# Sample rows' attention dealt out over the last 17 steps of a hybrid layer's main attention

## The reference

```python
(q, kv, gate, z_a, q_g, k_g, v_g, a_low, z_b, merge) = split(h @ w_in)
# prompt and sample rows alike:
o_nsa = gate0 * attend(q, compressed) + gate1 * attend(q, selected) + gate2 * attend(q, window)
# each head of the gated linear attention, chunks of 32 (prompt) or 4 (sample) tokens:
b = cumsum(log_sigmoid(a_low @ a_up + a_b) / 16)
q_dec, k_inv, k_tail = q * exp(b), k * exp(-b), k * exp(b_last - b)
o = tril(q_dec @ k_inv.T) @ v + q_dec @ S;  S = exp(b_last) * S + k_tail.T @ v
y = x + (sigmoid(g_a) * ((o_nsa * silu(z_a)) @ w_ba)
         + sigmoid(g_b) * ((rms_norm(o) * silu(z_b)) @ w_bb)) @ w_out
```

## Time and profile before

| | us |
|---|---|
| median of 3 runs | 1400.13 |
| lowest and highest | 1395.86, 1402.26 |
| profiled execution, its own time | 1407.33 |
| its span | 1405.3 |
| PE busy in the span | 1324.4 (94%) |
| DVE, ACT, POOL busy | 613.7 (44%), 621.4 (44%), 148.5 (11%) |
| mean granted TensorE clock | 0.974 of full |

### The profile page before, as it was taken

How to read it: one execution, slowest core, us unless ns; L and a number is a source line. 1 busy time by engine, 2 the same in 40 slices (tenths; PEclk the granted TensorE clock), 3 DMA queues, 4 the chain that set the end, 5 groups by cost and what they waited for, 6 DMA issues and landing times.

```text
span 1405.3 us, 23475 instructions
## 1 busy us (share of the span) xinstructions
PE 1324.4 (94%) x9533; PEld 1190.3 (85%) x9533; DVE 613.7 (44%) x1365; ACT 621.4 (44%) x1063; POOL 148.5 (11%) x182
## 2 busy tenths in 40 slices
PE   5999989998989999999999999999778889999998
PEld 4999989998978889988888899889556678999876
DVE  5211145634733344434333333332489766453342
ACT  5212235442332555655565567564558542221121
POOL 2100001103200000000000000001710270000000
PEclk9999999999989999999999999999779999999999
DMA  7251453411212212212122112212645555443231
GB/s 199 63 170 33 138 118 91 128 51 59 67 36 56 62 57 62 63 56 62 57 77 62 48 56 61 73 42 67 232 154 191 198 174 177 153 139 104 90 127 60
DMA packets 141307, 137.38 MB, mean 98 GB/s; under 512 B 27121, under 2 KB 125761, under 8 KB 141137
## 3 DMA queue, kind: packets, MB, share of 16 engines
q1 hardware_dynamic: 138416, 127.47, 29.8%
q0 software_dynamic: 2784, 8.43, 2.1%
HBM read 98.02 MB, written 41.88 MB: 100 GB/s over the span
## 4 chain that ended last, share of the span: by engine, by line
PE 65%; DVE 4%; ACT 2%; issue 2%; POOL 1%; DMA 1%; another core or an unknown queue 0%; POOLq 0%; SPq 0%; DVEq 0%; ACTq 0%
PE ps L218 37%; PE ps L2285 6%; PE ps L1176 5%; PE ps L1210 5%; PE ps L1192 4%; PE ps L1225 1%; PE ps L2196 1%; POOL oL L2334 1%; PE ps L2176 1%; DVE S L2392 1%; PE ps L2200 1%; PE ps L2293 1%; PE ps L1146 0%; DVE sP L1361 0%
## 5 line engine op out<-in xcount | busy, mean ns | idle before, releaser
L218 PE MATMUL ps<-hH,wH 128*128 128x352 f32 (+1 forms) x1320 | 443.0, 336 | 7.9 <-ACT stg L334 4.9
L218 PE MATMUL ps<-hH,wL 128*128 128x352 f32 (+1 forms) x1320 | 428.2, 324 | 0.0
L218 PE MATMUL ps<-hL,wH 128*128 128x352 f32 (+1 forms) x1320 | 427.5, 324 | 0.0
L218 PEld LDWEIGHTS ps<-hH,wH 128*128 128x128 f32 (+1 forms) x1320 | 250.0, 189 | 38.3 <-issue 26.9
L218 PEld LDWEIGHTS ps<-hL,wH 128*128 128x128 f32 (+1 forms) x1320 | 251.0, 190 | 2.2 <-issue 1.9
L218 PEld LDWEIGHTS ps<-hH,wL 128*128 128x128 f32 (+1 forms) x1320 | 250.0, 189 | 0.3
L1361 DVE CUSTOM_DVE_ANT_0 sP<-ps,dist,stat 128x256 f32<-128x256 f32 (+3 forms) x116 | 58.5, 542 | 203.4 <-issue 132.2
L205 DVE TENSOR_TENSOR wL<-w_raw,wH 128x1024 fp32r<-128x1024 f32 (+1 forms) x55 | 67.8, 1233 | 162.0 <-ACT wH L197 162.0
L1429 ACT ACTIVATE pPT<-ps 128x512 f32<-128x512 f32 x74 | 44.1, 596 | 181.2 <-PE ps L1192 181.1
L334 ACT ACTIVATE stg<-ps 128x352 f32<-128x352 f32 x132 | 60.8, 462 | 98.5 <-PE ps L218 90.0
L1472 ACT ACTIVATE sP<-sP,stat 128x640 f32<-128x640 f32 (+7 forms) x128 | 93.0, 729 | 4.4 <-DVE stat L1361 3.8
(11 more groups left out here) (378 smaller groups left out, 2100.8 us busy)
## 6 DMA issues: line engine op xcount, KB each, us to landing
w_raw<-in_w_in SPq DMA_DIRECT2D x46, 512.0 KB, 3.9
p_spill<-stg SPq DMA_DIRECT2D x132, 176.0 KB, 1.8
zt<-p_spill SPq DMA_DIRECT2D x24, 528.0 KB, 5.0
w_raw<-in_w_in SPq DMA_DIRECT2D x17, 256.0 KB, 3.8
gvT<-p_spill SPq DMA_DIRECT2D x8, 528.0 KB, 6.6
rq<-p_spill SPq DMA_DIRECT2D x8, 528.0 KB, 6.2
x_all<-in_x_prompt SPq DMA_DIRECT2D x8, 512.0 KB, 9.6
m_raw<-in_w_branch_b SPq DMA_DIRECT2D x8, 512.0 KB, 5.5
```

What stands on the lines that cost most here:

```text
L218: mm = nc.tensor.matmul(ps[0:t.m, bank, 0:NF], w[:, c % 2, t.m * k:t.m * k + t.m], x[:, k, NF * n:NF * n + NF], start=(k == 0 and i == 0), ...
```

## The change

The 93 units are dealt out over steps 0 to 48 instead of 0 to 65 (M0 = 49): 44 steps have two and five have one, where the before had 69 units in these 49 steps and 24 in the last 17. The sample rows' attention and head 0's elementwise part are no stage of their own any more:

- The two stages of the compressed branch go into steps 12 to 14 and 19 to 21 (C_AT), into columns 352 to 511 of the banks that the units use: `borrow` waits for the last unit's output, and `held` makes the second unit after it wait until DVE has read what was lent.
- The four stages with pages, the turning of pages, the gate products of heads 0 to 2 and head 0's elementwise part go into steps 49 to 65 (t = 0 to 16), in banks 2 and 3, which no unit needs there.
- In these 17 steps DVE's order is another one: a stage's bias, `copies(m)` with its `drain`, `output`, `weigh`, and only then `score(m+3)`, then a piece of head 0.
- The turning of head 0's values moves into `core(0)`, before its state products; SP loads these values after step 65's transposes. Page loads, biases, masks and the memory layout follow.

```diff
+                if u in held:
+                    pe.wait_ge(sem(held[u][0]), held[u][1])
                 ring.products(c, n, bank, hH, hL).then_inc(sem("u_done"), 1)
...
-            return UA * (m + 1) // ncut - UA * m // ncut
+            return UA * (m + 1) // M0 - UA * m // M0 if m < M0 else 0
...
+        M0 = 49
+        C_AT = (12, 19)
+        TURNS = {1: (1, 2), 2: (3,), 3: (4,), 5: (5, 6), 6: (7,), 7: (8,), 9: (9, 10), 10: (11,), 11: (12,), 13: (13, 14),
+                 14: (15,)}
...
+        def borrow(pe, what, u, read):
+
+            last = unit["pe"] - (1 if what == "scores" else 2)
+            unit_out(pe, last)
+            held[last + 2] = (read, u + 1)
+            lent[what, u] = 3 - last % 2
+            return lent[what, u]
...
+            def turn_page(c):
+
+                n, b = divmod(c, NB)
+                if b == 0:
+                    pe.wait_ge(sem(f"kp_loaded{n % 2}"), 16 * NB * (n // 2 + 1))
+                    if n >= 1:
+                        pe.wait_ge(sem("z_scored"), n + 2)
...
+                if t in (7, 11, 15):
+                    pe.wait_ge(sem("z_scored"), t // 4 + 3)
+                    decay_gate(pe, *((1, 0), (1, 2), (2, 1))[t // 4 - 1])
+                for c in TURNS.get(t, ()):
+                    turn_page(c)
+                if value_unit(t):
+                    turn_probs(value_unit(t))
...
+            def tail_step(m):
+
+                t = m - M0
+                if t % 4 == 3:
+                    z_score(score_unit(t - 1))
+                if value_unit(t):
+                    copy_probs(value_unit(t))
+                copies(m)
+                if value_unit(t):
+                    output(value_unit(t))
+                for j in range(4 * R):
+                    if cut_of[4 * j + 3, 0] == m:
+                        weigh(j)
+                if m + LA < ncut:
+                    score(m + LA)
+                head_part(t)
...
+                if m - 1 in C_AT:
+                    z_score(C_AT.index(m - 1))
+                if m - 2 in C_AT:
+                    copy_probs(C_AT.index(m - 2))
                 if m + LA < ncut:
                     score(m + LA)
+                if m - 2 in C_AT:
+                    output(C_AT.index(m - 2))
...
+            def tail_step(m):
+
+                t = m - M0
+                for c in TURNS.get(t, ()):
+                    copy_key(c)
...
+                copies(m)
...
+                if t % 4 == 3:
+                    z_probs(score_unit(t - 1))
+                if t == 3:
+                    log1p(act, 0)
```

More of the change, by code:

```diff
@@ L291, in hybrid_step @@
         NU = 3 * NP
+        held = {}
         unit = {"pe": 0, "act": 0, "dve": 0, "sp": 0}
@@ L1100, in hybrid_step @@
                 holder[spot[n] + k] = (n, k)
+        ZU = [(0, 2), (1, 2)] + [(gp, br) for gp in range(2) for br in range(2)]
+        PU = [(gp, br) for gp, br in ZU if br < 2]
+        cleared_free = list(cleared)
         UA = NU - 39
@@ new lines, in head_part @@
+            def head_part(t):
+                if t == 1:
+                    minus_abs(dve, 0)
+                elif t == 5:
+                    log_sigmoid(dve, link, 0)
+                elif t == 6:
+                    sums(dve, 0)
+                elif t == 7:
+                    tails(dve, link, 0)
+                elif t == 9:
+                    queries(dve, link, 0)
+                elif t == 10:
+                    inverses(dve, 0)
+                elif t == 11:
+                    keys(dve, link, 0)
+                elif t == 13:
+                    spans(dve, link, 0)
+                    for n in range(NSTG):
+                        dve.wait_ge(sem(f"p_stored{n}"), 16 * ((NU - n + NSTG - 1) // NSTG))
+                elif t == 14:
+                    later_queries(link, 0)
+                elif t == 15:
+                    minus_abs(dve, 1)
```

1131 lines of the change are left out of this document (571 added, 560 removed).

## The result

| kernel | median, us | runs | ratio to before | 95% interval |
|---|---|---|---|---|
| before | 1398.40 | 1395.86 to 1402.26, 4 runs | 1 | |
| changed | 1450.18 | 1440.69 to 1451.64, 4 runs | 1.0351 | 1.0307 to 1.0395 |

A forecast was written before the change was run, and what follows sets the result against it. PE was taken to bound the main attention, with units filling every wait. 91.7 + 117.7 + 17.2 = 226.6 us against 209.8, plus 17.2 for compressed stages and 7 for their clock, gave +41: 1441 us, range 1405 to 1456.

The forecast's parts named there:

- 24 units moved: Units leaving steps 49 to 65 become second units of earlier steps: 24 x 3.82 = 91.7 us.
- Compressed stages: Steps 12 to 14 and 19 to 21: 2.2 us of PE work plus three uncovered waits per stage, 17.2 us.
- The walk through the 17 steps: Steps 49 to 65 without units: 74 us PE work, 30 waits and 13 clock, 117.7 us.
- t = 3: Step 52: PE waits 3.8 us for ACT's copy, drain, score and bias before page 4 may overwrite the bank.
- t = 0: Step 49: PE waits 2.7 us while DVE makes a score, weigh and step 48's copy.
- t = 4: Step 53's transposes wait 1.3 us more, as the logarithm and two exponentials stand on ACT before them.
- The clock: Four waits in the last 17 steps are each followed by 6 to 10 us at 1.2 GHz, costing 13 us.
- The end: Step 65's transposes to the first state product: 17.2 us, PE waiting for head 0's values until 10.3; bounds 14 and 21.
- rival 3: Late loads and longer chains, with 12 us more for half clock: +57 to +65, about 1460 us; chance 8%.
- Drain at a table load: Logarithm's two table loads: a skill's 1.38 us drain each would add 2.8 us, making +44; left out of the forecast.
- Rival 1: PE's work alone counts, hand-overs hidden: 185 us against 210, -25, 1375 us; chance 9%.
- The signs: Window to step 49 about 526 + 24 us; 17 steps PE 75% busy, clock near 0.8, named idle times; above 0.95 wrong.

The follow-up runs named there:

- units_49: Kernel before with its projection units dealt over the first 49 steps, none in the last 17, sample stretch left in place; 1447.69 us, ratio 1.0325.
- c_out_first: Changed kernel with DVE doing the sample unit's output before the scores of step m+3 in steps 14 and 21; 1436.67 us, ratio 1.0233.
- c_ungated: Changed kernel with the compressed sample units at steps 25 and 32 instead of 12 and 19; 1442.71 us, ratio 1.0251.
- all4: Changed kernel with compressed units at steps 25 and 32, PE, DVE and ACT lists reordered, gated head's logarithm at t = 6 before spread weights' copy; 1400.52 us, 0.9987.
- log1p_late: Changed kernel with ACT's exponential and logarithm of the first gated head at the end of t = 4 instead of t = 3; 1452.94 us, ratio 1.0323.

## Why the prediction was right, point by point

Forecast 1441, measured 1450.18, in the range of 1405 to 1456 and on the forecast's side. By the trace of before, the forecast was a span of 1405.3 + 41 = 1446.3, and the changed kernel's trace has 1439.0, 7.3 less, of which 5.35 lie ahead of the first transposes, in code that did not change. So the forecast is 7 us too high between the two traces and 9 us too low at the median. The sum against the profiled execution of the changed kernel:

| term | forecast, us | trace after, us |
|---|---|---|
| first transposes to the last unit, with step 48's rest | 429.2 + 91.7 + 17.2 + 7 = 545.1 | 542.95 (404.11 to 947.06) |
| the 17 steps, to the last transposes | 117.7 | 114.6 |
| of them waits | 30 | 32.5 |
| of them clock | 13 | about 8 (114.6 - 32.5 - 74) |
| last transposes to the state product | 17.2 | 18.2 |
| everything behind | 356.8 | 359.2 |

- **24 units moved, 91.7.** Right. units_49 shows it alone: 517.97 us from the first transposes to the last unit, with 2.4 us of idle, where 429.2 + 91.7 less some 3 us of step 48 behind the last unit was forecast.
- **Compressed stages, 17.2, of which 15 are waits.** The three kinds were forecast as 2.9, 1.5 and 3.1 us and measured as 3.1, 1.4 and 3.2 on the mean. c_out_first and c_ungated each took one of them away. Not foreseen was the fourth (2.5 us at step 9): I had dealt with two units per step as with one.
- **The walk through the 17 steps.** The waits of t = 3 (3.8 forecast, 3.65 measured), t = 7 (6.4; 6.19) and t = 11 (2.2; 2.63) were right to half a microsecond. Three were too low: t = 0 (2.7; 3.84), t = 15 (1.1; 1.94) and t = 4 (1.3; 3.74), where the walk took half clock behind t = 3's wait to hide a part. No half clock came there in this execution. In that of c_ungated, with the same code there, it came, and the wait at t = 4 is 2.01. t = 10 and 12 were too high (3.1 and 2.7; 2.1 and 2.1). The list adds up by errors of both signs, so that 30 against 32.5 is in part luck.
- **The clock, 13.** The step that was mis-sized: about 8. I took the waits of t = 0, 3, 7 and 10 to be followed by 6 to 10 us at 1.2 GHz. In the profiled execution half clock follows those of t = 0, 4, 7 and 12, and for 3 to 5.5 us; none follows that of t = 10, nor the one before t = 3's page (3.65 us, ending at 974). Windows; the granted clock is the third number from the end:

```profile
1004.01:1009.50 5.49, 5.49 (x31) 4.78 (x33) 0.69 (x1) 2.26 (x5) 3.25 (x8) 0.50 0.51 143
1040.50:1043.50 3.00, 3.00 (x38) 2.56 (x41) 2.30 (x9) 0.00 (x0) 0.00 (x0) 0.50 0.00 0
960.00:982.00 22.00, 12.96 (x143) 9.23 (x139) 11.61 (x40) 12.11 (x24) 6.93 (x9) 1.00 0.23 73
```

  The first row stands behind the wait of t = 7, the second behind that of t = 12, the third holds that of t = 3. Over the 17 steps the granted clock is 0.93.

  The other three runs in the table's median are 9 to 11 us longer than the profiled one, with mean clocks of 0.965 to 0.970 against its 0.973. So the 9 us by which the forecast fell short of the median are of the size by which the executions differ, at clocks that differ too; no profile of such a run of the changed kernel exists, so where they lie is open.
- **The end.** Right as a sum (17.2; 18.2), by another way. Head 0's values were to be waited for until 10.3 us; their loads landed within 5.7 us and PE turned the values from 8.2 us on without a wait. In place of that wait come 4.6 us for ACT, which moves the turned values (0.25, 1.81, 1.77) and copies what the state product needs (0.78). Of the late loads of rival 3 nothing was seen.
- **Drain at a table load.** At t = 3 the load at 979.88 lasts 1.28 us and the exponential starts at 981.18, 0.02 us behind it, as in the kernel before:

```profile
978.78 1.08 ACT L1398 ACTIVATE ls<-ls 128x1056 f32<-128x1056 f32 x1
979.88 1.28 ACT L2122 ACT_TABLE_LOAD   x1
981.18 0.72 ACT L2122 ACTIVATE sP<-sP,stat 128x512 f32<-128x512 f32 x1
```

  The 2.8 us, an estimate from the drain that the Trainium skill (ScalarE: Activation LUTs, What ACT_TABLE_LOAD costs) states for each load, are not there: the logarithm ends at 979.86, so that 0.02 us lie ahead of the load too. 3.74 against 1.3 at t = 4 is not this term.
- **Rival 1** did not come: its 1375 us would have needed all waits hidden; even with the lists reordered the kernel reached 1400, with 11.8 us of gaps left in the 17 steps (all4).
- **The signs.** From step 0's first unit (398.64) to step 49 (947.06) it is 548.4 us, 526 + 24 forecast. PE is busy for 82.0 of 114.6 us (72%; 75% forecast). The named idle times are there, with the releasers named, but the second longest, t = 0's (3.84), was not named. The clock of 0.93 is nearer to the 0.95 that was to speak against the forecast than to its 0.8.

What the forecast did not see is that the two halves of the change stand so differently. I charged most of the 30 us to the dealt-out stages and their order of DVE; the bare steps alone, in the order of the kernel before, have 28.8 us of idle PE and cost as much.

## What to carry to other kernels

Before taking filler work away from a loop, walk its other engines' lists without it: an order that costs nearly nothing under a 4 us unit cost 1.3 us on the mean in ten of 17 steps here. In each list put first what the bottleneck waits for next, its operand copies and scores, and fill with long elementwise work only the places where that engine itself waits; then price such a change by the waits, not by totals, as DVE and ACT had the same work at 1450 and at 1400 us. When one wait is removed alone, expect part of it back at the next instruction, and judge the order as a whole.

## What the runs showed of the hardware

Code that is the same, with the same waits, ran at different lengths. log1p_late is the changed kernel up to t = 3; its stretch from the first transposes to the last unit, and behind it, from c_ungated, what follows the wait before t = 3's page:

```profile
406.78:952.33 545.55, 527.53 (x3870) 479.17 (x3868) 178.91 (x572) 263.37 (x439) 32.17 (x42) 0.98 0.21 61
```

```profile
972.50:977.90 5.40, 5.37 (x30) 4.50 (x32) 0.69 (x1) 3.97 (x6) 3.53 (x5) 0.50 0.60 156
```

Against the changed kernel's 540.05 us, 522.04 of them busy, the idle time is the same to 0.01 us (18.02 and 18.01), and PE's busy time differs by 5.5 us at a granted clock of 0.98 against 0.99. The same wait of 3.65 us at t = 3 was followed by half clock in c_ungated (second row), and by none in the changed kernel. So a wait costs its own length, which repeats from run to run to a hundredth (3.65, and 6.18 or 6.19, at t = 3 and 7 in the changed kernel, c_out_first, c_ungated and log1p_late), and a share of half clock behind it that does not. Single edits worth less than some 10 us are better judged by their waits in the trace than by medians of four runs.
